# Finishing the first modulation in two halves of the features

## What is computed

```python
def modulation(c, w, b):
    return jnp.split(jax.nn.silu(c) @ w + b, 3, axis=-1)

def sandwich(x, mod, g_pre, g_post, fn):
    shift, scale, gate = mod
    h = rms_norm(x, g_pre) * (1.0 + scale[:, None]) + shift[:, None]
    return x + gate[:, None] * rms_norm(fn(h), g_post)
```

## Time and profile before

| | us |
|---|---|
| median of three runs (1274.49 to 1278.53) | 1278.1 |
| the profiled execution | 1277.49 |
| its span in the trace | 1275.7 |
| TensorE busy | 1258.1 (99%) |
| VectorE busy | 924.4 (72%) |
| ScalarE busy | 719.6 (56%) |

### The profile page before, as it was taken

The page is one execution under the profiler, slowest core; times in us unless marked ns, Lnnn a source line. Parts: engine busy times, 40 slices in busy tenths (PEclk is TensorE's granted clock), DMA queues, the critical chain, the costliest instruction groups (busy, mean ns, idle before and its releaser), DMA issues.

```text
span 1275.7 us, 20877 instructions
## 1 busy us (share of the span) xinstructions
PE 1258.1 (99%) x8064; PEld 1142.6 (90%) x8064; DVE 924.4 (72%) x1183; ACT 719.6 (56%) x1069; POOL 51.3 (4%) x77
## 2 busy tenths in 40 slices
PE   8999999999999999999999999999999999999999
PEld 7998899999999778999989899888888888888887
DVE  6789978886899658666676676566666677666665
ACT  3586754444744557444466763655555667655554
POOL 1100000000111000000001000000000000000000
PEclk8899999999999999999999999999999999999999
DMA  9986989996799724556647544455566543366650
GB/s 350 350 312 199 343 279 327 339 328 203 242 363 376 232 49 165 198 198 199 201 160 224 175 141 135 132 197 198 200 201 203 187 164 97 117 217 205 202 165 33
DMA packets 147135, 274.46 MB, mean 215 GB/s; under 512 B 4759, under 2 KB 85423, under 8 KB 146936
## 3 DMA queue, kind: packets, MB, share of 16 engines
q1 hardware_dynamic: 132176, 220.21, 51.5%
q0 software_dynamic: 13648, 51.01, 11.9%
q10 hardware_dynamic: 1240, 2.26, 0.5%
HBM read 272.36 MB, written 1.10 MB: 214 GB/s over the span
## 4 chain that ended last, share of the span: by engine, by line
PE 87%; DVE 5%; DMA 4%; ACT 2%; issue 2%; ACTq 0%; POOL 0%; DVEq 0%; POOLq 0%
PE ps L2168 85%; DMA ada_ring<-in_ada_w 3%; DVE acc_a L1311 2%; DVE wlo L1294 1%; PE ps L2596 1%; ACT whi L541 1%; DMA voh<-in_voh 1%; PE ps L2324 1%; PE ps L2712 0%; ACT xn L598 0%; DVE x L1413 0%; DVE xn L1420 0%; PE ps L2905 0%; DVE hboth L2100 0%; ACT hboth L649 0%
## 5 line engine op out<-in xcount | busy, mean ns | idle before, releaser
L1294 DVE TENSOR_TENSOR wlo<-raw,whi 128x1024 fp32r<-128x1024 f32 x400 | 483.9, 1223 | 228.8 <-ACT whi L541 227.8
L541 ACT CAST whi<-raw 128x1024 fp32r<-128x1024 f32 x400 | 416.8, 1048 | 407.4 <-PE ps L2168 394.2
L2168 PE MATMUL ps<-hboth,whi 128*128 128x256 f32 (+1 forms) x2720 | 605.8, 311 | 1.4 <-DVE hboth L1478 1.0
L2168 PE MATMUL ps<-hboth,wlo 128*128 128x256 f32 x1792 | 491.5, 274 | 1.7 <-DVE hboth L1478 1.0
L2168 PEld LDWEIGHTS ps<-hboth,whi 128*128 128x128 f32 x2720 | 447.4, 191 | 30.5 <-issue 6.3
L2168 PEld LDWEIGHTS ps<-hboth,wlo 128*128 128x128 f32 x1792 | 343.9, 192 | 4.1 <-issue 1.9
L2168 PE MATMUL ps<-whi,hidhi 128*128 128x512 f32 x432 | 164.2, 380 | 0.0
L2168 PE MATMUL ps<-wlo,hidhi 128*128 128x512 f32 x432 | 163.7, 379 | 0.0
L2168 PE MATMUL ps<-whi,hidlo 128*128 128x512 f32 x432 | 163.7, 379 | 0.0
L2168 PE MATMUL ps<-whi,hboth 128*128 128x512 f32 (+1 forms) x512 | 155.7, 375 | 2.5 <-ACT att1o L872 0.8
L2168 PEld LDWEIGHTS ps<-whi,hboth 128*128 128x128 f32 x512 | 95.4, 190 | 18.4 <-issue 5.2
(11 more groups left out here) (251 smaller groups left out, 1127.0 us busy)
## 6 DMA issues: line engine op xcount, KB each, us to landing
raw<-in_ffn_w_in SPq DMA_DIRECT2D x44, 1024.0 KB, 7.0
ada_ring<-in_ada_w POOLq DMA_DIRECT2D x40, 1024.0 KB, 7.7
raw<-in_w_mlp_up SPq DMA_DIRECT2D x32, 1024.0 KB, 5.3
raw<-in_w_mlp_down SPq DMA_DIRECT2D x32, 1024.0 KB, 4.9
raw<-in_ffn_w_out SPq DMA_DIRECT2D x22, 1024.0 KB, 5.2
raw<-in_att_w_qkv SPq DMA_DIRECT2D x18, 1024.0 KB, 6.5
raw<-in_w_in_even SPq DMA_DIRECT2D x18, 1024.0 KB, 5.0
raw<-in_hyb_w_in SPq DMA_DIRECT2D x10, 1024.0 KB, 9.8
```

The source lines that it names most:

```text
L541: A.copy(whi[:, H % 4, :], raw[:, slot(n), h * HALF:(h + 1) * HALF]).then_inc(s["hi_ready"], 1)
L1294: V.tensor_tensor(wlo[:, H % 4, :], raw[:, slot(n), h * HALF:(h + 1) * HALF], whi[:, H % 4, :].bitcast(F32), ALU.subtract).then_inc(s["lo_ ...
L2168: return pe.matmul(out, lhsT, rhs, start=first, stop=last, skip_group_check=True)
```

## The change

The modulation's columns are loaded in the order 0, 1024, 512, 1536 (`ADA_COLUMNS`), so loads 0 to 3 hold shift and scale of features 0 to 511, loads 4 to 7 those of 512 to 1023. `x` is loaded second. Between loads 3 and 4 stand two loads of the projection: the lower row halves of its blocks 0 and 1; their upper row halves follow load 7. Slots and waits are renumbered for this. TensorE makes more of the products itself: `DIRECT` has two pieces of load 3 and 7, one of 4, 5 and 6.

TensorE drops all fillers but the first 12 and 8 ahead of the projection. Both token halves of `x` are scaled by ScalarE and turned by transposes (the products with the diagonal go). Then follow `ada_cols(3)`, sums 1, the fillers, and eight quarters in the order block 0 lower (2), block 1 lower (2), block 0 upper (2), block 1 upper (2). `ada_cols(4)`, `(5)` and `(6)` come after the second, third and fourth quarter, and after the fourth also sums 2, `ada_cols(7)` and sums 3. The upper column sums use bank 4.

`mod_cols(0, 0)` becomes `first_mod(0)` and `first_mod(1)`, four features' slices each. ScalarE makes both `h` and `hhi` of all eight slices (`first_pre`, two operations a slice; VectorE made four of the `h` before), VectorE the low parts (`first_low`). All splits up to half 7 stand among these, and `ada_first` 4 to 7 between the two halves; the splits of `proj` for block 0 on VectorE go. On ScalarE the table's copies move behind the norms, splits 8 to 11 move before the two evacuations. Left out of the diff below are the renumbered waits on `mod_ready` and `h32_ready`, the body of `ada_first` (its `parts` argument) and ScalarE's loop over the first blocks, which now runs splits 8 and 9, evacuation 0, splits 10 and 11, evacuation 1.

```diff
@@ -282,13 +282,21 @@
         def xn_of(j):
             return (xn1, h321) if j < 4 else (xn2, h322)
+        def ring(n):
+            return n + 4 if 0 <= n < 2 else n + ADA_FIRST
+        def ada_ring_at(a):
+            return a if a < 4 else a + 2
         def slot(n):
-            return (n + ADA_FIRST) % RAW
+            return ring(n) % RAW
         def in_count(n):
-            return 16 * ((n + ADA_FIRST) // RAW + 1)
+            return 16 * (ring(n) // RAW + 1)
         ada_flat = ada_ring[:, :, :, :].rearrange("p a b c -> p (a b c)")
         pt2, yd = ada_flat[:, 0:20 * P], ada_flat[:, 20 * P:20 * P + S]
@@ -330,7 +338,8 @@
             return 0 if lv == NM - 1 else 4 + 2 * (lv % 2)
-        DIRECT = {6: (3,), 7: (2, 3)}
+        ADA_COLUMNS = (0, 1024, 512, 1536)
+        DIRECT = {3: (2, 3), 4: (3,), 5: (3,), 6: (3,), 7: (2, 3)}
         DVE_LAST, PE_LAST = (4, 5), (6, 7)
...
@@ -373,17 +382,31 @@
         @block.sync
         def _(sp):
+            def after_ada(a):
+                sp.wait_ge(s["ada_used"], a + 1)
+                if a in DIRECT:
+                    sp.wait_ge(s["ada_pe"], sorted(DIRECT).index(a) + 1)
+            def load_ada(a):
+                if a >= 4:
+                    after_ada(a - 4)
+                ap, k = src_cols(t["ada_w"][0, 0], ADA_COLUMNS[a // 2], a % 2)
+                at = ada_ring_at(a) % RAW
+                sp.dma_start(raw[:, at, :].rearrange("p (k n) -> p k n", k=k), ap).then_inc(raw_in[at], 16)
             def load(n, it, src):
                 ap, k = src
                 if isinstance(it, int) and EARLY <= n < FIRST["ffn0"]:
                     sp.wait_ge(s["lo_ready"], 2 * (n - EARLY) + 2)
-                if n >= RAW:
+                if n >= RAW + 2:
                     sp.wait_ge(s["lo_ready"], 2 * (n - RAW) + 2 + 12 * it)
-                elif n + ADA_FIRST >= RAW:
-                    sp.wait_ge(s["ada_used"], n + ADA_FIRST - RAW + 1)
-                    if n + ADA_FIRST - RAW in DIRECT:
-                        sp.wait_ge(s["ada_pe"], n + ADA_FIRST - RAW - 5)
+                elif n >= 4:
+                    after_ada(n)
+                elif n >= 2:
+                    sp.wait_ge(s["lo_ready"], 2 * (n - 2) + 2)
                 dst = raw[:, slot(n), :].rearrange("p (k n) -> p k n", k=k)
                 sp.dma_start(dst, ap).then_inc(raw_in[slot(n)], 16)
...
@@ -415,11 +438,17 @@
                         load(n + 1 + 2 * g, 0, src_up(wi, (g + 1) * GW))
                     load(n + min(2 + 2 * g, 2 * NG2 - 1), 0, src_down(wo, g * GW))
-            for a in range(ADA_FIRST):
-                load(a - ADA_FIRST, 0, src_cols(t["ada_w"][0, 0], (a // 2) * 512, a % 2))
-                if a == 3:
-                    sp.dma_start(x[:, :, :], t["x"][0].rearrange("(t p) n -> p t n", p=P)).then_inc(s["x_in"], 16)
-            proj(FIRST["hyb_in"], t["hyb_w_in"][0], HYB)
+            load_ada(0)
+            sp.dma_start(x[:, :, :], t["x"][0].rearrange("(t p) n -> p t n", p=P)).then_inc(s["x_in"], 16)
+            for a in range(1, 4):
+                load_ada(a)
+            for n in range(2):
+                load(n, 0, src_cols(t["hyb_w_in"][0], HYB[n][1], 0))
+            for a in range(4, ADA_FIRST):
+                load_ada(a)
+            for n in range(2, 4):
+                load(n, 0, src_cols(t["hyb_w_in"][0], HYB[n - 2][1], 1))
+            proj(FIRST["hyb_in"] + 4, t["hyb_w_in"][0], HYB[2:])
             for c in range(4):
                 load(FIRST["hyb_out"] + c, 0, src_down(t["hyb_w_out"][0], c * 2 * P))
...
@@ -776,26 +805,41 @@
             tables(LN_EXP)
             act.wait_ge(s["one_ready"], 1)
+            norms(0)
+            act.wait_ge(s["vec_dil"], 1)
+            A.copy(vrow[:, 3 * VLEN_DIL:], ps[0:8, 7, :]).then_inc(s["vec_dil_c"], 1)
+            act.wait_ge(s["root_x"], 2)
+            act.wait_ge(s["ssq_x"], 4)
+            A.activation(xn1[:, 0, :], x[:, 0, :], ACT.Copy, scale=small[:, 5, 3:4]).then_inc(s["xn_ready"], 1)
+            A.activation(xn1[:, 1, :], x[:, 1, :], ACT.Copy, scale=small[:, 5, 4:5]).then_inc(s["diag_ready"], 1)
             for g in range(3):
-                act.wait_ge(s["vec_dil"], g + 1)
-                A.activation(vrow[:, g * VLEN_DIL:(g + 1) * VLEN_DIL], ps[0:8, 4 + g, 0:VLEN_DIL], ACT.Copy,
+                act.wait_ge(s["vec_dil"], g + 2)
+                A.activation(vrow[:, g * VLEN_DIL:(g + 1) * VLEN_DIL], ps[0:8, 1 + g, 0:VLEN_DIL], ACT.Copy,
                              scale=1.0 / DIL_SCALE).then_inc(s["vec_dil_c"], 1)
-            act.wait_ge(s["vec_dil"], 4)
-            A.copy(vrow[:, 3 * VLEN_DIL:], ps[0:8, 7, :]).then_inc(s["vec_dil_c"], 1)
             act.wait_ge(s["vec_dil_c"], 4)
             act.dma_start(t["vec_dil"].rearrange("g h n -> h g n"),
                           vrow[:, 0:3 * VLEN_DIL].rearrange("h (g n) -> h g n", g=3)).then_inc(s["vec_out"], 16)
             act.dma_start(t["vec_swa"], vrow[:, 3 * VLEN_DIL:]).then_inc(s["vec_out"], 16)
-            norms(0)
-            act.wait_ge(s["root_x"], 1)
-            act.wait_ge(s["ssq_x"], 2)
-            A.activation(xn1[:, 0, :], x[:, 0, :], ACT.Copy, scale=small[:, 5, 3:4]).then_inc(s["xn_ready"], 1)
-            act.wait_ge(s["const_in"], 48)
-            act.wait_ge(s["root_x"], 2)
-            A.activation(diag[:, :], ident[:, :], ACT.Copy, scale=small[:, 5, 4:5]).then_inc(s["diag_ready"], 1)
-            split(0)
-            pre(0)
+            def first_pre(parts):
+                for k in parts:
+                    if k >= 4:
+                        act.wait_ge(s["hlo_ready"], k - 3)
+                    A.activation(h32_slot(0, k), turned_ps(0, k), ACT.Identity, bias=shcol[:, 0, k:k + 1],
+                                 scale=scol[:, 0, k:k + 1])
+                    A.activation(hhi[:, k, :], turned_ps(0, k), ACT.Identity, bias=shcol[:, 0, k:k + 1],
+                                 scale=scol[:, 0, k:k + 1]).then_inc(s["hhi_ready"], 1)
+            act.wait_ge(s["turned"], 8)
+            for half in range(2):
+                split(4 * half)
+                act.wait_ge(s["mod_ready"], half + 1)
+                first_pre((4 * half, 4 * half + 1))
+                split(4 * half + 1)
+                first_pre((4 * half + 2, 4 * half + 3))
+                split(4 * half + 2)
+                split(4 * half + 3)
             act.wait_ge(s["lb_step"], 1)
...
@@ -1346,7 +1401,23 @@
                 V.scalar_tensor_tensor(out=scol[:, j, :], in0=scol[:, j, :], scalar=1.0,
                                        in1=col("g_pre", 8 * j, 8), op0=ALU.add, op1=ALU.mult) \
                     .then_inc(s["mod_ready"], 1)
-                dve.wait_ge(s["mod_ready"], j + 1)
+                dve.wait_ge(s["mod_ready"], j + 2)
+            def first_mod(half):
+                k, bank = 4 * half, 4 * half
+                dve.wait_ge(s["cols_sum"], 2 * half + 2)
+                V.tensor_tensor(shcol[:, 0, k:k + 4], ps[:, bank, 0:4], col("b_shift", k, 4), ALU.add)
+                link(V.tensor_tensor(scol[:, 0, k:k + 4], ps[:, bank, 4:8], col("b_scale", k, 4), ALU.add))
+                V.scalar_tensor_tensor(out=scol[:, 0, k:k + 4], in0=scol[:, 0, k:k + 4], scalar=1.0,
+                                       in1=col("g_pre", k, 4), op0=ALU.add, op1=ALU.mult) \
+                    .then_inc(s["mod_ready"], 1)
+            def first_low(k):
+                dve.wait_ge(s["hhi_ready"], k + 1)
+                V.tensor_tensor(hlo[:, k, :], h32_slot(0, k), hhi[:, k, :].bitcast(F32), ALU.subtract) \
+                    .then_inc(s["hlo_ready"], 1)
...
@@ -1637,15 +1708,33 @@
             V.tensor_tensor(stat[:, 8:12], col("lb", 0, 4), col("lb", 0, 4), ALU.subtract).then_inc(s["lb_step"], 1)
             dve.wait_ge(s["sil_c"], 1)
-            for a in range(4):
-                ada_first(a)
+            ada_first(0)
             mean_x(0, 0)
             mean_x(0, 1)
-            for a in range(4, ADA_FIRST):
+            for a in range(1, 4):
                 ada_first(a)
-            mod_cols(0, 0)
+            first_mod(0)
             split(0)
-            pre(0)
+            first_low(0)
+            first_low(1)
+            split(1)
+            first_low(2)
+            ada_first(4, (0,))
+            first_low(3)
+            split(2)
+            ada_first(4, (1, 2))
+            split(3)
+            for a in range(5, ADA_FIRST):
+                ada_first(a)
+            first_mod(1)
+            split(4)
+            first_low(4)
+            first_low(5)
+            split(5)
+            first_low(6)
+            first_low(7)
+            split(6)
+            split(7)
             lbt = small[:, 4, :]
             dve.wait_ge(s["lb_act"], 1)
...
@@ -2414,7 +2502,8 @@
                 pe.wait_ge(s["ada_used"], 2 * nb + 2)
                 for i in range(4 * nb, 4 * nb + 4):
-                    m = mm(ps[:, 0, i:i + 1], acc_a[:, i * P:(i + 1) * P], ones[:, 0:1], i == 0, True)
```

(44 more changed lines are left out.)

32 lines of the change are left out of this document (21 added, 11 removed).

## The result

| | kernel before | changed kernel |
|---|---|---|
| median of nine runs each, side by side | 1276.29 (1274.49 to 1278.56) | 1280.78 (1279.15 to 1282.07) |
| ratio to the kernel before | | 1.0036 [1.0024, 1.0048] |
| ratio, measured a second time (e8) | | 1.0029 [1.0013, 1.0044] |
| profiled execution | 1277.49 | 1279.15 |

The account below looks back on a forecast made before the run. It took TensorE's line, with VectorE's nearly equally late up to 94 us, to bound the kernel. Profiled 1277.5 plus 2.2 for VectorE's later arrival gave 1279.7, on the median's scale 1280.3; range 1276 to 1286.

Parts of the forecast that it names:

- My favourite: Whole kernel: the outcome given the highest chance, a change of no more than 0.3% (3.8 us) either way; 0.64.
- I take the low clock: TensorE's first half: 48 sums and transposes at 0.213 us, 10.2 in all; modulation ready at 28.3, projection start at 31.0.
- rival 3: TensorE's turn (transposes): the clock rises there, first half ends 4.2 us earlier, total -0.5 to -3.3 us; chance 0.13.
- the main case: Both lines up to the return at 94 us: VectorE's delay makes the kernel +1 to +3.3 us slower; chance 0.50.
- The 10 us come from the dropped fillers: Ahead of the projection: start at 31.0 instead of 41.3 because 60 + 8 + 8 + 4 + 4 fillers go, not through overlap.
- The overlap is paid for in TensorE's own queue: TensorE between the lower quarters: 6.3 us of column work moves there, making the upper modulation late, ready at 48.7.
- VectorE's line: VectorE behind the upper modulation: splits and low parts until 56.9, gate modulation at 57.8 against 54.26, 3.5 us later.
- The third ring block: Gate modulation on VectorE: waits for a further ring transfer and starts at 79.3 to 81.4, against 78.20.
- The bound: Kernel before, up to 94 us: TensorE's and VectorE's lines nearly equally late, the chain running through VectorE and ring transfers 52 to 94.
- The step from profile to median: Final sum: the profiled execution lies 0.6 us under the median shown, so 1279.7 becomes 1280.3.
- Rival 2: Before the `bandqk` matmuls: band transfers arrive late, TensorE waits 3.7 us, total +4.6 to +8 us; chance 0.30.
- Rival 4: VectorE's line has more slack than its rows show; only TensorE's +0.9 us or less remains, 1278 to 1279; chance 0.07.

Follow-up runs that it names:

- e8: The changed kernel timed and profiled again without any edit; ratio to the kernel before 1.0029 [1.0013, 1.0044].
- e9: The kernel before, timed and profiled again without any edit: 1275.01 us, 0.9995 [0.9979, 1.0012].
- e12: Changed kernel with the gate modulation's first transfer and four products early, splits 4 to 6 ahead of the upper modulation, 5 fillers in TensorE's gap: 1275.40 us, 0.9994.
- e2: Changed kernel with 30 fillers given back, 14 at the start and 16 ahead of the first column sums: 1280.7 us, 1.0029.
- e6: Changed kernel with two pieces, of loads 4 and 5, given back from TensorE to VectorE: 1280.6 us, 1.0036.
- e3: Kernel before with VectorE's first three gate modulation blocks cut to 16 of 512 columns: 1274.78 us, 0.9987.
- The light pair: Kernel before and changed kernel, both with VectorE's first three gate modulation blocks cut to 16 of 512 columns: 1274.78 us (0.9987) and 1276.93 us (0.9999).
- e5: Changed kernel with the gate modulation's first transfer issued after four loads and its four products ahead of the upper modulation on VectorE: 1277.01 us, 1.0010.
- e11: Changed kernel with splits 4, 5 and 6 ahead of the upper modulation and five fillers behind the last column sums: 1277.27 us, 1.0005.
- e4: Changed kernel with VectorE's first three gate modulation blocks cut to 16 of 512 columns: 1276.93 us, 0.9999.
- e10: Changed kernel with splits 4, 5 and 6 moved ahead of the upper modulation on VectorE and ScalarE: 1278.13 us, 1.0021.

## Why the prediction was right and wrong

The direction, the range (1280.78 in 1276 to 1286) and the place were right. My favourite, within 0.3%, was missed by a little: 0.36%, and 0.29% the second time; both intervals lie on both sides of 0.3%. **That 1280.3 is only 0.5 us off is luck.** The difference was forecast at +2.2 (+1 to +3.3) and is 4.5, or 3.7 the second time; the base was put 1.7 us too high (1278.1 for 1276.4), and the two errors cancel. The steps one by one:

- **Loads: right.** `x` landed at 10.99 (forecast 11.4), the second lower weight load at 24.64 (25.0), `ada` 7 at 35.43 (35.9).
- **"I take the low clock" for the first half: wrong in this execution.** 28.3 was forecast, 24.81 measured; the 24 one-column instructions behind the turn cost 0.115, not 0.213. By the sign that the prediction names, a clock at full before 27, this is rival 3, which I gave 0.13. What it was to bring (-0.5 to -3.3) didn't come in the time. On the profile that my sum stood on the lines are there: VectorE's level at 54.33 (forecast 0.3 ahead), TensorE's 2.1 ahead at 60.43 (forecast 3.3), the return of the chain at 94.79 against 94.42, where the main case had 96 to 97.5. But that before was a late one. In three of the nine traces the low clock held as I had taken it. The Trainium skill (TensorE: Matmul & The Clock Gate, Part 4, PE-mode transpose) says transpose mode doesn't count as work for the clock's gate. By it the clock stays low through the turn, as in three of the nine traces; in the six others it rises right behind the turn or a few sums later, so here the rule doesn't tell which comes. What holds is the price at each level, and that both happen.
- **"The 10 us come from the dropped fillers": wrong.** e1 takes 42 of them from before and moves the projection by 0.8 us at most and the time by nothing. The 31.0 itself came from a sum over the new order and doesn't rest on this sentence.
- **"The overlap is paid for in TensorE's own queue": right**, and the core of it. 27.35 to 44.9 is 17.6 us for four quarters and the column work (forecast 17.0), then 2.19 idle (2.4), then 2.7 lost at the low clock (2.4). Against e9 TensorE starts 11.1 us sooner and has 6.3 of column work, 2.2 of waiting, 2.7 of low clock behind the gap and 0.3 of low clock at the projection's start more: 0.4 later at 60.43, forecast +0.9. e12 shows the same without the ring's loop.
- **VectorE's line: right in its working.** From the upper modulation to the gate modulation I had 9.1 us (48.7 to 57.8), measured 9.29 (45.04 to 54.33). The absolute times are 3.5 early, as the clock's rise made the whole half early. Against e9 it is 2.6 later, forecast 3.5.
- **The third ring block: bound right, middle too low.** The transfer took 9.65 us (9.33 in e8, 9.27 in the earlier trace rows), and no trace has the 7.2 of the lower end: the fastest for this block took 8.41 (e2) and 8.66 (e6). So the lower part of 79.3 to 81.4 was empty. At the return to TensorE the shift is 2.8 to 3.1 against e9 (94.50, 94.79; 91.66), where I took 2.2 of 1.1 to 3.2.
- **The bound: wrong for the kernel before.** The earlier trace rows showed VectorE's line and TensorE's nearly level. In e9, and in e1 and e3, TensorE's is alone. It didn't hurt the difference much, for the changed kernel stands on VectorE's line; but it hid that **the change moves the bound**, from TensorE to a chain of products, splits and transfers. The light pair (1.7 against 4.7 us) and e5, which changes VectorE's order and the issue of one transfer and brings 2.6 per mille, show it.
- **The step from profile to median: wrong by 1.7 us, and it hid a miss of 2.2.** I put the profiled execution 0.6 under the median of three; with 29 runs the median is 1276.4 and that execution 1.1 above it. On the right base my +2.2 would have given 1278.6; of the 2.2 that are missing 0.6 to 0.9 are the ring, 0.1 to 0.4 the growth of the delay between 94 and 150 us, and the rest isn't placed (see what stays open).
- **Rival 2, band transfers late: wrong for the changed kernel, by 2.3 us of room.** On ScalarE's timeline of the changed kernel they were issued 0.2 us after the first upper slice began, landed by 58.1 and were wanted at 60.4:

```profile
45.50 0.56 ACT L829 ACTIVATE h<-ps,shcol,scol 128x256 f32<-128x256 f32 x1 [6.30 <-DVE scol L1412]
45.67 0.36 ACTq L848 DMA_DIRECT2D masks<-in_masks  x1
...
51.94 0.24 ACT L845 ACTIVATE stat<-stat 128x4 f32<-128x4 f32 x1
```

An operation that precedes the issue in the program ran at 51.94, so the sequencer was some 12 instructions ahead. The estimate of 50 from the queue of 8 that the Trainium skill (TensorE: Matmul & The Clock Gate, opening table) gives ScalarE came to the right verdict on this rival, which the recorded text there calls the third; the rows show the sequencer further ahead than that. How thin the room is, e6 shows: there the landing, not the issue, was late, and TensorE waited 1.73.

- **Rival 4 (VectorE's slack): wrong.** The changed kernel's third block waits 2.91 us for its transfer.

**What stays open.** From 358 to 411 us the ring's transfers pace both kernels, and this stage's length varies from execution to execution with no order by kernel. From the start of the first block to the second half of the fifth it is 47.1 us in e2, 47.4 in the first profile of before, 47.6 in e5, 48.3 after, 48.8 in e9, 49.3 in e12, 50.1 in e8 and 50.5 in e11. From its first to its fifth first-piece operation on VectorE, before (e9) and changed (e8):

```profile
358.72 0.48 DVE L1308 TENSOR_SCALAR acc_a<-ada_ring,sc 128x512 f32<-128x512 f32 x1
...
403.88 0.49 DVE L1308 TENSOR_SCALAR acc_a<-ada_ring,sc 128x512 f32<-128x512 f32 x1
```

```profile
362.00 0.48 DVE L1361 TENSOR_SCALAR acc_a<-ada_ring,sc 128x512 f32<-128x512 f32 x1 [0.25 <-DMA ada_ring<-in_ada_w]
...
408.43 0.48 DVE L1361 TENSOR_SCALAR acc_a<-ada_ring,sc 128x512 f32<-128x512 f32 x1
```

45.2 us against 46.4. That is why the spans of two profiles (1274.0 and 1278.3) differ by more than the 3.0 us at 150, and I don't put it down to the change. Its cause wasn't tried. Nor are the 1 to 1.5 us settled by which the median's 4.5 exceed the delay at 334 us; the second comparison, 0.29% or 3.7 us, leaves less. A likely place for them is the clock: both profiles of the changed kernel are at 0.991, and its executions at 0.989 have medians of 1281.0 (8) and 1280.2 (5), those at 0.991 1279.2 (1) and 1278.9 (4). e4 and e5, at 0.989, show what such an execution can look like, low from 43.3 to 53.6; the changed kernel itself was never profiled in it.

## What to carry to other kernels

An early start is worth what the queue behind it doesn't take back: list the work that moves in between and the wait that appears at the second half, and see which line is then the last; here 11 us of head start went to 6.3 of column work, 2.2 of waiting and 3.0 of low clock, and the delayed second half came back some 3 us late through a ring of transfers that had been just in time. If work must be halved like this, put what doesn't depend on the second half (gate products, splits) ahead of its wait, on every engine; that gave over half of it back by itself (e5), and with a few fillers in the gap all of it (e12), but nothing beyond. When an edit gains less than expected, measure it from the event that it stands behind: e5's and e10's worth is plain from the upper modulation on and hidden in the absolute times. And take two profiles of the kernel before, or hold the one against the median of more than three runs, before two lines in it are called level.
